# Two attentions as one sequence, heads turned in two places, and other work moved in a four-layer transformer kernel

## The chip, the cores and the metric

The kernel runs on one core of a Trainium2 chip. The metric is the device time of one execution in microseconds. The kernel before took 1555.3 us (median of 3 runs, 1555.01 to 1556.13).

The engines are named as in the profile: PE is TensorE's matmul, PEld its weight load, DVE is VectorE, ACT is ScalarE, POOL is GpSimd, SP is SyncE, which here issues the DMAs.

## The reference, cut to what matters

Four layers run on one sequence of 512 rows of width 1024, in float32. The first two have 256 rows of context beside them and are modulated; the last two each add a gated per-layer embedding.

```python
def ab_layer(...):                                   # layer 1: rows and context together
    h, gate = adaln(x, mod)                          # rmsnorm(x) * (1 + scale) + shift; mod = silu(c) @ mod_w + mod_b
    qa, ka, va, qb, kb, vb, g = heads_ab(h @ w_in, *wts)   # qa, ka = rmsnorm(.., q_gain), rmsnorm([kv[:64], kr], k_gain)
    qa, ka = rope_tail(qa, 32, row, col), rope_tail(ka, 32, row, col)
    qb, kb = axial_rope(qb, row, col), axial_rope(kb, row, col)
    oa = joint_dense_attention(qa, ka, va, kac, vac)  # "mla": 8 heads, 64 + 32 wide; the last 32 of each key are one shared kr
    ob = joint_dense_attention(qb, kb, vb, kbc, vbc)  # "gqa": 8 heads of 64, 2 key heads
    x = x + gate * ((concat(oa, ob) * silu(g)) @ w_out)
# layer 2 ("win"): window attention with a sink, and a short convolution; same frame
# layer 3: 4 heads of a difference of two softmaxes ("diff"), 4 heads with forget gates ("fox"), causal
# layer 4: 8 heads, softmax over a dilated causal pattern ("odd")
def per_layer_embedding(h, p_i, w_ple, w_gate):
    return h + (p_i @ w_ple) * jax.nn.sigmoid(h @ w_gate)
```

## The kernel before, in words

Each engine has its program written out by hand; waits are on semaphores that count up, so an instruction that waits holds up all behind it on its engine. No scheduler moves anything.

A matrix product of two float32 operands is made of three: each operand is split into a high part, rounded to the PE's faster format, and the low rest, and high x high, high x low and low x high are added (L1048 to L1050). ACT makes the high part of a weight tile (L1445) and POOL the low part (L2353), while PE multiplies by the tile before. The rows to be multiplied are turned by PE against a unit matrix (L1004), ACT copies the high part out of PSUM (L1517) and DVE takes the low part (L1959). `turns_at` says beside which weight tile each 128-column slab is turned. Stages follow each other: `in1`, `up`, gqa, mla, `out1`, `in2`, win, `out2`, `in3`, diff and fox, `out3`, `sig3`, `ple3`, `in4`, odd, `out4`, `sig4`, `ple4`.

**Column attention** (gqa, mla, win) goes over units j, one head and one tile of 128 rows each (48, 48 and 32 units). In place j PE makes the scores of unit j (L1269 to L1274), turns what heads are due (L1215, `prep`), turns the probabilities of unit j - 2 (L1236), and in every second place multiplies those of units j - 4 and j - 3 by the values (L1293). DVE finds the maximum (L2093), ACT takes the exponential (L1594), and both copy the turned probabilities out of PSUM (L1610 on ACT, L2104 on DVE). A turned query pair of gqa or win is copied by ACT in two halves (L1572) and its low part taken by DVE in two halves (L2027), all in one place. gqa's places run to 51, the last four without scores, and only then begins mla's place 0. The first head of mla is turned in gqa's last 8 places, and the first of these turns waits until POOL has normed all of mla's queries and keys (`ready_of`, L2400 to L2468).

**mla's norms.** POOL squares each of the six key tiles (L2392, 128x768), DVE sums each (L2252) between its other work of gqa's first six places; there is one buffer for the squares, so the two take turns. The queries' squares and sums are DVE's alone, before gqa. After the root (in gqa's places 6 to 9) POOL multiplies the queries by root and gain and rotates them, then the keys.

**Modulation.** 32 column tiles of `mod_w` are multiplied beside `in1` (L1151) and turned back (L1159), two for each weight tile; ACT copies the results in `mod_columns`. The gates that come of them are spread over a tile by PE (L1168, `spread_at`) in stated places.

**Layer 3** runs its 32 units in `pair_attention`: scores of unit n (L1364, L1371) in PSUM banks 0 and 1 or 2 and 3 by turns, probabilities of unit n - 3 (L1391), values of unit n - 4 (L1401). It begins with a wait for all values of diff and fox; `attention`, for layer 4, likewise. In two late places of fox, slabs 0 and 1 of `m3`, the operand of `out3`, are turned (`late_turn`), slabs 2 to 7 beside `out3`'s first three weight tiles.

Of the kernel before, what the change touches and what calls it, by code (L numbers as in the profile page):

```python
# [108 lines left out]
def build(nc, io, out, known):  # L109
# [22 lines left out]
    with ctx:  # L132
# [145 lines left out]
        def mod_tile(n_):  # L278

            return rx[:, n_ % 4, :].rearrange("p (k m) -> p k m", k=KT)  # L280

        def mod_row(n_):

            return rx[:, NX, n_ % 2 * P:(n_ % 2 + 1) * P]

        def mods_beside(n_):

            return (2 * n_ - 8, 2 * n_ - 7) if 4 <= n_ < 4 + len(MOD) // 2 else ()
# [63 lines left out]
        def lo_of(u):  # L352
# [3 lines left out]
                     ("win", 3): (1, 0, 0), ("win", 9): (1, 0, 1)}  # L356
# [50 lines left out]
        for name, t_ in (("in2", "h2"), ("out3", "m3"), ("out4", "m4")):  # L407
            for u in range(-1 if t_[0] == "h" else 0, 3):
                turns_at[name, 0, u] = [(t_, 2 * u + 2, 2 * u + 4, XT) if t_ == "h2" else (t_, 2 * u + 2, 2 * u + 4)]
# [7 lines left out]
        late_turns = {"fox": "m3", "odd": "m4"}  # L417

        def late_turn(name, j):
# [3 lines left out]
            groups = groups_of(late_turns[name], 0, 2)  # L423
            n_ = j - (len(units_of(name)) - 1 - len(groups))
# [10 lines left out]
        for name in turn:  # L435
            for k in range(turn[name]["slabs"]):
# [3 lines left out]
                for i, g in enumerate(turn[name]["groups"]):  # L440
                    if name[0] == "m" and k < 2:
                        bank_of[name, k, g[0]] = 7
                        continue
# [149 lines left out]

        def pair_done(name, p_):

            return ("mixed", (name, (p_ + 1) * (4 if name == "win" else 6) - 1))
# [15 lines left out]
        def pair_probs(n_, m, a, b):  # L612

            if PAIR[n_][0] == "fox":
                return both_low[:, 2 + n_ % 4, a:b]
            return both[:, 2 * (n_ % 4) + m, a:b]

        def pair_bank(n_):

            return 1 if PAIR[n_][0] == "fox" and n_ % 2 else 6  # L620

# [52 lines left out]
        def prep_times(name):  # L674
# [3 lines left out]
            for p_ in preps:  # L678
# [84 lines left out]
        def heads_view(ap, h):  # L763
            return ap.rearrange("p (h d) -> p h d", h=h)

# [105 lines left out]
        def _(eng):  # L871
# [60 lines left out]
            for m, u in enumerate(first_two[4:], 4):  # L932
# [4 lines left out]
                for n_ in mods_beside(m - 2):  # L937
# [52 lines left out]
        def _(eng):  # L990
# [154 lines left out]
            def modulation_tile(n_):  # L1145

                eng.wait_ge(*at(f"load_mod{n_ % 4}", n_))
                bank_free(7)
                for k in range(KT):
                    q = 32 * (k % 4)  # L1150
                    mm = eng.matmul(psum[q:q + 32, 7, 0:P], silu_pad[:, k, :], mod_tile(n_)[:, k, :], start=k < 4, stop=k >= 4)  # L1151
                mm.then_inc(*to("mod_product", n_))
                reader[7] = ("mod_rows", n_)

            def turn_modulation(n_):

                eng.wait_ge(*at("mod_rows", n_))
                bank_free(7)
                eng.matmul(psum[:, 7, 0:2], mod_row(n_), sel[:, :], start=True, stop=True).then_inc(*to("mod_turned", n_))  # L1159
                reader[7] = ("mod_columns", n_)  # L1160
# [22 lines left out]
            def running_sums():  # L1183
# [11 lines left out]
                "gqa": [("keys_twice", ("gqa", 1))] + [("vector", ("normed", "gq", t)) for t in ALL],  # L1195
                "mla": [("gpsimd", ("normed", n_, t)) for n_ in ("mq", "mk") for t in ALL] + [evac_of("up3", t) for t in ALL],
                "win": [("keys_twice", ("win", 1))] + [("vector", ("normed", "wq", t)) for t in XT],
# [5 lines left out]
            def prep(name, p_):  # L1203

                key, _, rows, tiles, _, d = p_
                if p_[0] == prep_times(name)[-1][0][0]:
                    for w_ in ready_of[name]:
                        eng.wait_ge(*at(*w_))
                if name == "odd" and key[1] == 4:
                    for t in XT:  # L1210
                        eng.wait_ge(*at("vector", ("normed", key[0] + "1", t)))
                b, m_ = prep_bank(name, p_), turned_rows(name, p_)
# [4 lines left out]
                reader[b] = copied(name, p_)  # L1217

# [27 lines left out]
            def column_attention(name):  # L1246
                units, preps = units_of(name), prep_times(name)
                n_units, waited = len(units), set()
                for j in range(n_units + 3):
                    if j < n_units:  # L1250
                        h, t = units[j]
                        wait_heads(name, j, waited)
# [29 lines left out]
                    if 2 <= j < n_units + 2:  # L1282
                        turn_probs(name, j - 2, probs(name, j - 2))
                    m, r = divmod(j - 4, 2)
# [1283 lines left out]
```

## Time and profile before

| what | value |
|---|---|
| median of 3 runs | 1555.3 us |
| the profiled execution's own time | 1554.78 us |
| its span | 1553.0 us |
| PE busy | 1487.5 us, 96% |
| PEld busy | 1240.5 us, 80% |
| DVE, ACT, POOL busy | 850.9, 677.9, 592.3 us |
| mean granted TensorE clock | 0.998 |
| chain that ended last: PE, DVE, POOL, ACT | 81%, 7%, 5%, 3% |

The span runs from the program's first instruction to its last, and 1.8 us of the execution lie around it. Busy is time in which at least one instruction of the engine is under way. PE is idle for 1553.0 - 1487.5 = 65.5 us; the rest of this document is about where.

### The profile page before, as it was taken

How to read it: one execution, taken by the hardware profiler on the slowest of the kernel's cores; microseconds unless marked ns; L12 is line 12 of the kernel's file. 1: busy time of each engine (PE TensorE's matmuls, PEld its weight loads, DVE VectorE, ACT ScalarE, POOL GpSimd, SP SyncE). 2: the span in 40 equal slices, each digit the busy share in tenths (PEclk: the TensorE clock that was granted, in tenths of full speed). 3: DMA queues.
4: the chain of work that ended last, by engine and by line, in shares of the span. 5: the costliest groups of instructions: out<-in, count | busy, mean ns of one | idle time of the engine just before them, and what ended most of it. 6: DMA issues, size and time to landing. Idle time of an engine off the chain costs nothing.

```text
span 1553.0 us, 25078 instructions
## 1 busy us (share of the span) xinstructions
PE 1487.5 (96%) x9488; PEld 1240.5 (80%) x9488; DVE 850.9 (55%) x1879; ACT 677.9 (44%) x1377; POOL 592.3 (38%) x349
## 2 busy tenths in 40 slices
PE   4999998898999999999899999999999999999998
PEld 3778787787888878888788889967788788877887
DVE  4573708876764265933742997056322599617322
ACT  3333336565566353335744333467323433346332
POOL 1212223691005553447725444423234444430244
PEclk9999999999999999999999999999999999999999
DMA  9657620000012333331013323300233233310322
GB/s 326 181 140 192 175 62 27 2 2 1 2 35 89 108 109 96 95 95 42 28 33 94 96 82 98 93 14 28 69 93 106 75 99 101 96 41 1 109 82 95
DMA packets 103717, 128.61 MB, mean 83 GB/s; under 512 B 10608, under 2 KB 63792, under 8 KB 103600
## 3 DMA queue, kind: packets, MB, share of 16 engines
q1 hardware_dynamic: 103600, 127.01, 27.4%
q8 instruction: 78, 1.28, 0.4%
q14 instruction: 39, 0.32, 0.1%
HBM read 124.90 MB, written 2.10 MB: 82 GB/s over the span
## 4 chain that ended last, share of the span: by engine, by line
PE 81%; DVE 7%; POOL 5%; ACT 3%; issue 3%; DMA 1%; SPq 1%; DVEq 0%; ACTq 0%; POOLq 0%
PE psum L1048 21%; PE psum L1050 20%; PE psum L1049 20%; PE psum L1293 3%; PE psum L1236 3%; PE psum L1004 2%; PE psum L1215 2%; PE psum L1151 1%; PE psum L1340 1%; PE psum L1322 1%; PE psum L1272 1%; POOL rx L2403 1%; POOL mla_q L2403 1%; DVE psum L1943 1%; PE psum L1273 1%
## 5 line engine op out<-in xcount | busy, mean ns | idle before, releaser
L2353 POOL TENSOR_TENSOR wlo<-wraw,whi 128x1024 fp32r<-128x1024 f32 (+4 forms) x181 | 413.1, 2283 | 704.6 <-ACT whi L1445 704.6
L1445 ACT ACTIVATE whi<-wraw 128x1024 fp32r<-128x1024 f32 (+4 forms) x181 | 181.6, 1003 | 421.7 <-PE psum L1050 415.4
L1048 PE MATMUL psum<-whi,h2h 128*128 128x512 f32 (+2 forms) x800 | 309.5, 387 | 2.6 <-DVE h2l L1959 1.5
L1050 PE MATMUL psum<-whi,h2l 128*128 128x512 f32 (+2 forms) x800 | 305.2, 382 | 0.0
L1049 PE MATMUL psum<-wlo,h2h 128*128 128x512 f32 (+2 forms) x800 | 304.6, 381 | 0.0
L1048 PEld LDWEIGHTS psum<-whi,h2h 128*128 128x128 f32 x800 | 150.3, 188 | 28.5 <-issue 2.7
L1050 PEld LDWEIGHTS psum<-whi,h2l 128*128 128x128 f32 x800 | 150.2, 188 | 27.1
L1049 PEld LDWEIGHTS psum<-wlo,h2h 128*128 128x128 f32 x800 | 150.4, 188 | 24.8
L1048 PE MATMUL psum<-whi,hTh 128*128 128x512 f32 (+2 forms) x372 | 143.4, 385 | 3.7 <-DVE hTl L1959 2.7
L1050 PE MATMUL psum<-whi,hTl 128*128 128x512 f32 (+2 forms) x372 | 136.2, 366 | 0.0
L1049 PE MATMUL psum<-wlo,hTh 128*128 128x512 f32 (+2 forms) x372 | 135.8, 365 | 0.0
L1048 PE MATMUL psum<-hTh,whi 128*128 128x512 f32 (+1 forms) x288 | 109.0, 379 | 0.8 <-ACT rz L1501 0.8
L1049 PE MATMUL psum<-hTl,whi 128*128 128x512 f32 (+1 forms) x288 | 105.6, 367 | 0.0
L1050 PE MATMUL psum<-hTh,wlo 128*128 128x512 f32 (+1 forms) x288 | 105.4, 366 | 0.0
L2093 DVE TENSOR_REDUCE nmax<-psum 128x1 f32<-128x768 f32 (+1 forms) x96 | 74.9, 780 | 49.6 <-PE psum L1274 28.2
L1048 PEld LDWEIGHTS psum<-whi,hTh 128*128 128x128 f32 x372 | 70.5, 189 | 18.0 <-POOL wlo L2353 4.6
L1594 ACT ACTIVATE pr<-psum,nmax 128x768 f32<-128x768 f32 (+3 forms) x96 | 64.1, 667 | 39.2 <-DVE nmax L2093 23.7
L1050 PEld LDWEIGHTS psum<-whi,hTl 128*128 128x128 f32 x372 | 70.3, 189 | 11.5
L2364 POOL TENSOR_TENSOR hTl<-rz,hTh 128x768 fp32r<-128x768 f32 (+1 forms) x12 | 19.7, 1647 | 156.4 <-ACT hTh L1616 156.4
L1049 PEld LDWEIGHTS psum<-wlo,hTh 128*128 128x128 f32 x372 | 70.7, 190 | 9.1
L1959 DVE TENSOR_TENSOR h2l<-psum,h2h 128x512 fp32r<-128x512 f32 x32 | 22.0, 691 | 86.0 <-ACT h2h L1517 85.9
L1236 PE MATMUL psum<-ident,pr 128*128 128x128 f32 x368 | 58.8, 277 | 6.1 <-ACT prT L1610 1.8
(391 smaller groups left out, 2956.4 us busy)
## 6 DMA issues: line engine op xcount, KB each, us to landing
rx<-mod_w_in SPq DMA_DIRECT2D x32, 512.0 KB, 5.1
wraw<-w_in_odd_in SPq DMA_DIRECT2D x32, 512.0 KB, 3.6
wraw<-cd_w_in_in SPq DMA_DIRECT2D x24, 512.0 KB, 3.7
wraw<-w_in_even_in SPq DMA_DIRECT2D x20, 512.0 KB, 3.7
wraw<-ab_w_out_in SPq DMA_DIRECT2D x16, 512.0 KB, 3.7
wraw<-w_ple_gate_in SPq DMA_DIRECT2D x16, 512.0 KB, 3.8
mod_w_even<-mod_w_in SPq DMA_DIRECT2D x8, 512.0 KB, 10.3
wraw<-ab_w_in_in SPq DMA_DIRECT2D x8, 512.0 KB, 8.3
```

Source lines behind the costliest of these rows:

```text
L1004: mm = eng.transpose(psum[:, b, n_ * P:(n_ + 1) * P], turn[name]["rows"](t, k), ident[:, :])
L1048: eng.matmul(dst, a[0], ww[0], start=first, stop=False)
L1049: eng.matmul(dst, a[0], ww[1], start=False, stop=False)
L1050: mm = eng.matmul(dst, a[1], ww[0], start=False, stop=last_)
L1215: mm = eng.transpose(psum[0:m_, b, n_ * P:(n_ + 1) * P], rows(t), ident[:, :])
L1236: mm = eng.transpose(psum[:, bk, (b - b0) * P:(b - b0 + 1) * P], place[:, b * P:(b + 1) * P], ident[:, :])
L1293: eng.matmul(psum[64 * e:64 * e + 64, 6, 0:P], v_rows(name, h + e, b), turned_probs(name, 2 * m + e)[:, n_ * P:(n_ + 1) * P], start=n_ == ...
L1445: eng.activation(hi_of(u)[:, :, 0:w], wraw[:, u["id"] % RAW, :, 0:w], ACT.Copy).then_inc(*to("split_hi", u["id"]))
L1594: eng.activation(place[:, 0:w], psum_flat[:, s0 * 512:s0 * 512 + w], ACT.Exp, bias=nmax[:, j % 4:j % 4 + 1], scale=-1.0, accum_out=rsum[:, ...
L2093: eng.tensor_reduce(m, sc, AX.X, ALU.min).then_inc(*note("nmax", (name, j)))
L2353: eng.tensor_tensor(lo_of(u)[:, :, 0:w], wraw[:, u["id"] % RAW, :, 0:w], f32(hi_of(u)[:, :, 0:w]), ALU.subtract)\
L2403: eng.tensor_tensor(view(t), view(t), gg, ALU.mult).then_inc(*(small() if turned else note("gpsimd", ("normed", name, t))))
```

## The change

In the order of the program:

- **Modulation.** The last two of the 32 column tiles leave `in1`; they are multiplied in gqa's places 0 and 1 and turned back in places 1 and 2. `mod_columns` is split into `mod_rows` and `mod_columns`.
- **First heads.** A head's turn waits for its own norms: gqa's and win's keys for `keys_twice` alone, mla's keys and queries each for their own.
- **mla's norms.** The shared 32 columns of a key are squared once; the other 64 of 8 heads in twelve pieces of 128x256 with two buffers, of which DVE sums two in each of six places. The gain of the keys' first 64 columns is multiplied into the queries' gain, so POOL multiplies only 32 columns of each key head by a gain (128x256 in place of 128x768). Keys are normed before queries.
- **One sequence.** gqa and mla form one list of places: mla's place 0 follows gqa's place 47. Heads 2 and 3 of mla are turned in places 3 to 10 (before: 0, 1, 3, 4, 6, 7, 9, 10).
- **Pairs.** The second half of a turned query pair is copied and its low part taken one place after the first.
- **Gate.** Layer 2's gate, second half, is spread in win's place 6 (before: 9).
- **Values.** diff, fox and odd wait for their values just ahead of the first product with them.
- **fox.** Its scores go through banks 0, 2 and 3. Slabs 0 to 3 of `m3` are turned in four late places, slabs 4 to 7 beside `out3`'s first two weight tiles.

```diff
         def mods_beside(n_):
-            return (2 * n_ - 8, 2 * n_ - 7) if 4 <= n_ < 4 + len(MOD) // 2 else ()
+            return mod_pair(n_) if n_ < 19 else ()
...
         spread_at = {("gqa", 5): (0, 0, 0), ("gqa", 7): (0, 0, 1), ("gqa", 9): (0, 1, 0), ("gqa", 21): (0, 1, 1),
-                     ("win", 3): (1, 0, 0), ("win", 9): (1, 0, 1)}
+                     ("win", 3): (1, 0, 0), ("win", 6): (1, 0, 1)}
...
+        for u in range(2):
+            turns_at["out3", 0, u] = [("m3", 2 * u + 4, 2 * u + 6)]
...
-        late_turns = {"fox": "m3", "odd": "m4"}
+        late_turns, EARLY_SLABS = {"fox": "m3", "odd": "m4"}, {"m3": 4, "m4": 2}
...
+        def places(*names):
+            return [(name, j) for name in names for j in range(len(units_of(name)) + 4 * (name == names[-1]))]
...
+        def pair_scores(n_):
+            return 2 * (n_ % 2) if PAIR[n_][0] == "diff" else (0, 2, 3)[(n_ - 16) % 3]
...
-                    when = first + (3 * before // 2 if name == "mla" else 2 + 2 * before)
+                    when = first + (max(3 * before // 2, 3 + before if first == 0 else 0) if name == "mla" else 2 + 2 * before)
...
+            def start_modulation(j):
+                if j < 2:
+                    modulation_tile(30 + j)
+                if j > 0:
+                    turn_modulation(29 + j)
...
-                if p_[0] == prep_times(name)[-1][0][0]:
+                if name in STACKED and key[1] == 0:
+                    for w_ in [("keys_twice", (name, 1))] if key[0] == "k" else [("vector", ("normed", name[0] + "q", t)) for t in tiles]:
+                        eng.wait_ge(*at(*w_))
+                elif p_[0] == prep_times(name)[-1][0][0]:
...
+                if name == "mla" and key[1] == 0:
+                    for t in tiles:
+                        eng.wait_ge(*at("gpsimd", ("normed", "m" + key[0], t)))
...
                         bl = blocks_of(name, t)
+                        if i == 0:
+                            values_ready(name)
                         copies_ready(name, i)
...
             def column_attention(*names, beside):
...
                     if j < len(units_of(name)):
                         maximum(name, j)
+                    for what in preps_at(name, j - 1) if j else ():
+                        low(*what, which=(1,))
                     for what in preps_at(name, j):
-                        low(*what)
+                        low(*what, which=(0,))
...
             def mla_norms():
...
+                eng.tensor_tensor(shared_squares, kr[:, :, :], kr[:, :, :], ALU.mult).then_inc(*note("squares_g", ("kr", 0)))
+                for n_ in range(2 * NT):
...
+                    eng.tensor_tensor(key_squares(n_), rows, rows, ALU.mult).then_inc(*note("squares_g", ("mk", n_)))
                 eng.wait_ge(*at("vector", ("root", "mla")))
-                for name, roots in (("mq", heads_rstd[:, 0:48]), ("mk", heads_rstd[:, 48:96])):
+                for name, roots in (("mk", heads_rstd[:, 48:96]), ("mq", heads_rstd[:, 0:48])):
...
-            column_attention("gqa")
-            column_attention("mla")
+            column_attention("gqa", "mla")
```

What this makes of the instructions' order is shown at three places. PE at gqa's start, before (kTs and qTs are gqa's turned keys and queries, gq its rows, pr the probabilities):

```order
L1269 MATMUL psum<-kTs,qTs 128x512
L1270 MATMUL psum<-kTs,qTs 128x512
L1269 MATMUL psum<-kTs,qTs 128x256
L1270 MATMUL psum<-kTs,qTs 128x256
L1269 MATMUL psum<-kTs,qTs 128x512
L1270 MATMUL psum<-kTs,qTs 128x512
L1269 MATMUL psum<-kTs,qTs 128x256
L1270 MATMUL psum<-kTs,qTs 128x256
L1269 MATMUL psum<-kTs,qTs 128x256
L1270 MATMUL psum<-kTs,qTs 128x256
L1215 MATMUL psum<-ident,gq 128x128 x4
L1236 MATMUL psum<-ident,pr 128x128 x6
```

and now, from the end of the first unit's scores:

```order
L1323 MATMUL psum<-kTs,qTs 128x256
L1186 MATMUL psum<-rx,silu_pad 32x128 x8
L1322 MATMUL psum<-kTs,qTs 128x512
L1323 MATMUL psum<-kTs,qTs 128x512
L1322 MATMUL psum<-kTs,qTs 128x256
L1323 MATMUL psum<-kTs,qTs 128x256
L1186 MATMUL psum<-prT,silu_pad 32x128 x8
L1195 MATMUL psum<-sel,prT 128x2
L1322 MATMUL psum<-kTs,qTs 128x256
L1323 MATMUL psum<-kTs,qTs 128x256
L1262 MATMUL psum<-ident,gq 128x128 x4
L1195 MATMUL psum<-sel,prT 128x2
```

The two modulation tiles (L1186) and their turns (L1195) stand among the first three units' scores. ACT a few instructions later, before (more_q is a turned query pair's place, prT and rx the turned probabilities):

```order
L1594 ACTIVATE pr,rsum<-psum,nmax 128x768 x2
L1572 ACTIVATE more_q<-psum 64x512 x2
L1610 ACTIVATE prT<-psum 128x512
L1594 ACTIVATE rx,rsum<-psum,nmax 128x256
L1610 ACTIVATE prT<-psum 128x512
L1594 ACTIVATE pr,rsum<-psum,nmax 128x256
L1572 ACTIVATE more_q<-psum 64x256 x2
```

and now:

```order
L1770 ACTIVATE modc<-psum,mod_b 128x2
L1628 ACTIVATE more_q<-psum 64x512
L1666 ACTIVATE prT<-psum 128x512
L1650 ACTIVATE rx,rsum<-psum,nmax 128x256
L1628 ACTIVATE more_q<-psum 64x512
L1666 ACTIVATE prT<-psum 128x512
L1650 ACTIVATE pr,rsum<-psum,nmax 128x256
L1628 ACTIVATE more_q<-psum 64x256
L1650 ACTIVATE pr,rsum<-psum,nmax 128x768
L1628 ACTIVATE more_q<-psum 64x256
```

Each second half now stands behind an exponential and a copy. PE at the end of gqa, before (kTh, kTl, qTh, qTl are mla's turned keys and queries, high and low; the products with the values that stand between are left out):

```order
L1215 MATMUL psum<-ident,mla_q 96x128 x2
L1236 MATMUL psum<-ident,pr 128x128 x12
...
L1298 MATMUL psum<-ident,rinv 64x128 x2
L1236 MATMUL psum<-ident,rx 128x128 x6
...
L1272 MATMUL psum<-kTh,qTh 128x512
```

and now:

```order
L1262 MATMUL psum<-ident,mla_q 96x128 x2
L1289 MATMUL psum<-ident,pr 128x128 x6
L1325 MATMUL psum<-kTh,qTh 128x512
L1326 MATMUL psum<-kTl,qTh 128x512
L1327 MATMUL psum<-kTh,qTl 128x512
...
L1289 MATMUL psum<-ident,pr 128x128 x6
...
L1354 MATMUL psum<-ident,rinv 64x128 x2
```

mla's first scores stand between the turned probabilities of gqa's last units.

## Rows read from the trace of the kernel before

**Rows 1.** Busy time by stretch: length, busy of each engine, clock, DMA.
```profile
262.00:294.00 32.00, 24.83 (x214) 20.33 (x216) 26.81 (x58) 17.56 (x40) 11.50 (x9) 1.00 0.01 2
```

**Rows 2.** Waits of PE, whole span: us in total, times, longest.
```profile
PE psum L1215 <- DVE nlam L2235: 1.6, 1, 1.6
...
PE psum L1048 <- DVE h2l L1959: 1.5, 1, 1.5
PE psum L1215 <- POOL rx L2403: 1.4, 1, 1.4
PE psum L1364 <- ACT buf L1501: 1.4, 1, 1.4
...
PE psum L1322 <- ACT buf L1501: 1.3, 1, 1.3
...
PE psum L1168 <- DVE kTw L2027: 1.1, 1, 1.1
```

**Rows 3.** Timeline of PE in in1: start, us, what, idle before.
```profile
197.37 0.40 PE L1049 MATMUL psum<-hTl,whi 128*128 128x512 f32 x1
197.60 0.40 PE L1050 MATMUL psum<-hTh,wlo 128*128 128x512 f32 x1
197.93 0.64 PE L1151 MATMUL psum<-rx,silu_pad 128*32 128x128 f32 x16
198.50 0.38 PE L1048 MATMUL psum<-hTh,whi 128*128 128x256 f32 x1
```

**Rows 4.** Timeline of DVE ahead of gqa's first maximum.
```profile
259.45 2.31 DVE L2027 TENSOR_TENSOR qTs<-psum,qTs 64x512 fp32r<-64x512 f32 x4
263.10 0.96 DVE L2093 TENSOR_REDUCE nmax<-psum 128x1 f32<-128x768 f32 x1 [1.33 <-PE psum L1270]
```

**Rows 5.** Groups of DVE, 262 to 294: busy, mean ns, idle before.
```profile
L2252 DVE TENSOR_REDUCE ssq<-squares 128x8 f32<-128x768 f32 x6 | 5.7, 953 | 1.9 <-POOL squares L2392 1.5
...
L2093 DVE TENSOR_REDUCE nmax<-psum 128x1 f32<-128x256 f32 x4 | 1.7, 425 | 0.4
```

**Rows 6.** Timelines of DVE and of POOL beside each other in in3.
```profile
864.67 0.69 DVE L1857 TENSOR_REDUCE ssq<-squares 128x8 f32<-128x512 f32 x1
865.46 1.98 DVE L1855 TENSOR_TENSOR squares<-buf 128x512 f32<-128x512 f32 x1
...
864.13 2.76 POOL L2353 TENSOR_TENSOR wlo<-wraw,whi 128x1024 fp32r<-128x1024 f32 x1 [3.55 <-ACT whi L1445]
```

**Rows 7.** Timeline of PE: a wait in gqa, two in win.
```profile
308.68 1.01 PE L1236 MATMUL psum<-ident,rx 128*128 128x128 f32 x6 [0.64 <-ACT prT L1610]
...
750.72 0.52 PE L1236 MATMUL psum<-ident,win_pr 128*128 128x128 f32 x3 [0.89 <-ACT gate L1610]
...
760.57 0.41 PE L1236 MATMUL psum<-ident,win_pr 128*128 128x128 f32 x2 [0.71 <-ACT win_prT L1610]
```

**Rows 8.** Groups of POOL, 250 to 355.
```profile
L2403 POOL TENSOR_TENSOR rx<-rx,gains 128x768 f32<-128x768 f32 x6 | 11.0, 1826 | 0.5
...
L2392 POOL TENSOR_TENSOR squares<-rx 128x768 f32<-128x768 f32 x6 | 8.8, 1467 | 17.2 <-DVE ssq L2252 17.2
...
L2461 POOL TENSOR_TENSOR squares<-rx,grid 128x128 f32<-128x128 f32 x4 | 1.8, 457 | 0.3
```

**Rows 9.** Waits of PE, 371 to 387, from gqa's end into mla.
```profile
PE psum L1293 <- DVE rz L2123: 1.1, 1, 1.1
PE psum L1272 <- ACT pr L1594: 0.6, 1, 0.6
PE psum L1236 <- ACT prT L1610: 0.6, 1, 0.6
```

**Rows 10.** Timelines of POOL and PE: sub-norms' end, fox's twelfth scores' end.
```profile
1082.94 1.28 POOL L2450 TENSOR_TENSOR rz<-rz 128x512 f32<-128x512 f32 x1
...
1085.24 0.22 PE L1373 MATMUL psum<-mask_right,mask_left 128*128 128x128 f32 x1
```

**Rows 11.** Busy time by stretch, near the start.
```profile
26.00:29.00 3.00, 3.00 (x9) 2.31 (x9) 0.00 (x0) 1.06 (x1) 0.14 (x1) 0.50 1.07 361
```

More of the change, by code:

```diff
@@ L1244, in copies_ready, with column_attention @@
                     eng.wait_ge(*at("probs_b", (name, i)))
[L1246 to L1250, printed above, removed]
+            def column_attention(*names):
+                seq, waited = places(*names), {name: set() for name in names}
+                for n_, (name, j) in enumerate(seq[:-1]):
+                    units = units_of(name)
+                    if j < len(units):
                         h, t = units[j]
-                        wait_heads(name, j, waited)
+                        wait_heads(name, j, waited[name])
                         s0 = score_bank(j)
@@ L1345, in pair_attention @@
             def pair_attention():
-                for name in ("diff", "fox"):
-                    for n_ in values_of[name]:
-                        for t in XT:
-                            eng.wait_ge(*at(*evac_of(n_, t)))
                 waited = set()
@@ L1571, in prep @@
                 for e, (rows, hi, _) in enumerate(parts_of(name, p_)):
+                    if e not in which:
+                        continue
                     eng.activation(hi, shaped(psum[rows, prep_bank(name, p_), 0:len(tiles) * P], hi), ACT.Copy)\
@@ L1616, in mix_hi, with column_attention @@
                 eng.activation(hi, m, ACT.Copy).then_inc(*to("mix_hi", (name, p_)))
[L1618 to L1620 removed]
+            def column_attention(*names):
+                seq = places(*names)
+                if "gqa" in names:
+                    mod_rows(30)
+                for n_, (name, j) in enumerate(seq):
+                    units = units_of(name)
                     if (name, j - 1) in spread_at:
                         spread(*spread_at[name, j - 1])
+                    for what in preps_at(name, j - 1) if j else ():
+                        prep(*what, which=(1,))
                     for what in preps_at(name, j):
[L1624 to L1626 removed]
+                        prep(*what, which=(0,))
+                    if 2 <= n_ < len(seq) - 2:
+                        copy_probs(*seq[n_ - 2], turned_probs(*seq[n_ - 2]), product_of(seq[n_ - 5]) if n_ >= 5 else None)
                     if j < len(units):
[L1628 to L1629 removed]
+                        if n_ >= 3:
+                            probs_free(*seq[n_ - 3])
                         exponentials(name, j, probs(name, j))
+                    if name == "gqa" and j < 2:
+                        if j == 0:
+                            mod_rows(31)
+                        mod_columns(30 + j)
                     if (name, j) in LEADS:
@@ L1757, in _ @@
             products("in1", "up", beside=tables)
-            column_attention("gqa")
-            column_attention("mla")
+            column_attention("gqa", "mla")
             def first_squares(where):
@@ L2104, in copy_probs, with column_attention @@
                 eng.tensor_copy(place[:, 0:nb * P], psum[:, 4, 0:nb * P]).then_inc(*note("probs_a", (name, i)))
-            def column_attention(name, beside=lambda j: None):
-                units, preps = units_of(name), prep_times(name)
-                for p_ in preps[-1] if name == "win" else ():
-                    first_head(name, p_)
-                for j in range(len(units) + 4):
-                    if j < len(units):
+            def column_attention(*names, beside):
+                seq = places(*names)
+                for p_ in prep_times("win")[-1] if "win" in names else ():
+                    first_head("win", p_)
+                for n_, (name, j) in enumerate(seq):
+                    if j < len(units_of(name)):
@@ L2129, in column_attention @@
-                    beside(j)
+                        eng.reciprocal(rinv[:, r_:r_ + 2], rsum[:, c_:c_ + 2]).then_inc(*note("vector", ("inverse", name2, m)))
+                    if name != "mla":
+                        beside(j)
             def attention(name):
@@ L2283, in _ @@
                     first_head("gqa", p_)
-            column_attention("gqa", mla_norms)
-            column_attention("mla")
+            column_attention("gqa", "mla", beside=mla_norms)
             products("out1", 0)
@@ L2306, in conv @@
                        .then_inc(*note("conv", ("lo", c)))
-            column_attention("win", conv)
+            column_attention("win", beside=conv)
             products("out2")
```

170 lines of the change are left out of this document (104 added, 66 removed).

## The prediction

> **What bounds the kernel now.** I read the page's busy shares first: PE is busy for 1487.5 of 1553.0 us, so all that moving work about can win is the 65.5 us in which it is idle, and what stands in PE's way as surplus. Next the mean clock, 0.998: nearly everything runs at the upper level. Next the busy time by stretch, to find the idle time. It isn't in the weight products but at the borders of the attentions, and the worst stretch is the first 32 us of gqa, where PE is busy for 24.8 us and DVE for 26.8 [rows 1]: there DVE sets the pace. Last the waits of PE, whose single large ones [rows 2] I take one by one, since the change names most of them.
>
> **The change part by part.** Each term is a gain of PE's time.
>
> *Modulation and first heads.* A modulation tile in `in1` stands between starts at 197.60 and 198.50, where two matmuls follow each other after 0.23 us: 0.90 - 0.23 = 0.67 us of PE [rows 3]. Two tiles leave, 1.3 us; their turns, a matmul of two columns each, I count at nothing. In gqa's places 0 and 1 the tiles cost nothing, as PE waits there for DVE and ACT. ACT's two copies and two column results fall between exponentials that wait for maxima. The first turn of gqa's keys no longer waits for the queries' norms, 1.6 us [rows 2]. But both come to PE's queue before gqa, and ahead of the first scores DVE has a chain of its own, which ends with the low part of the queries at 259.45 + 2.31 = 261.76 and is then idle for 1.33 us, until the first maximum [rows 4]. That chain is led by work that follows PE in `up`, so it moves with the 1.3 us. Of the 1.6 us only what lies between 261.76 and the scores' start is left: two matmuls of 512 and two of 256 columns and a hand-over take about 1.0 of the 1.33 us, so 0.3. Term: 1.6 us. Bounds: 0.3 if DVE's chain doesn't move, 2.9 if it is no limit.
>
> *mla's norms at gqa's start.* DVE waited 1.5 us in all for POOL's squares [rows 5]; with two buffers POOL works ahead. Its pieces of 256 columns take between 0.46 and 1.47 us [rows 8], two in each place, so 2.9 us at most where a place of this stretch takes over 2. DVE sums twelve pieces at 0.43 (the price of a 128x256 reduction) = 5.1 us in place of 5.7, and adds one more sum and one addition, at most 0.43 each, and six more hand-overs at about 0.07 ((1.9 - 1.5) / 6) = 0.4 [rows 5]. So 1.5 + 0.6 - 0.7 - 0.4 = 1.0 us. Bounds: 0 and 2.
>
> What could eat this is POOL itself, which now squares while DVE sums; before, one buffer kept them apart. In `in3` both occur beside each other: with POOL at work from 864.13 to 866.89, DVE's product of two tiles in SBUF takes 1.98 us, until about POOL's end, while its reduction in the same stretch takes 0.69 [rows 6]. The Trainium skill, page "SBUF — State Buffer", section on the shared port pair, has it that a VectorE instruction with two SBUF inputs and a GpSimd instruction that reads SBUF shut each other out for their whole length, and that a reduction on trn2 never contends; the trace agrees. By the rule alone the twelve sums keep their 0.43 us. Were it wrong, each sum would wait for up to a piece of POOL's.
>
> *POOL's chain.* PE waits 1.4 us for it at mla's first turn [rows 2]. Twelve gain products of 1.83 us stood in the chain; six shrink to 256 columns, between 0.46 and 1.83 us each [rows 8], and nearest to 0.7 by a straight line: the chain is 6 x 1.1 = 6.8 us shorter. Keys come first and only they are waited for in gqa's place 40. The whole 1.4 us goes. Bounds: 0.9 and 1.6. Next late is the PSUM bank between the turns, which is not changed.
>
> *The seam.* From gqa's end into mla PE waits 1.1 us for DVE's mixing, 0.6 for ACT's copy and 0.6 for the first exponential of mla [rows 9]. They come of draining one list and filling another. In one sequence mla's scores stand between gqa's last turned probabilities, so 2.3 us go. Against it mla's turns for heads 2 and 3 now fall in eight places in a row, which hand one bank on each time: I give back 0.4. Term 1.9. Bounds: 0 and 3.
>
> *Pairs.* Where a query pair is copied in two halves the turned probabilities stand behind 1.2 us of ACT. PE waited 0.64, 0.89 and 0.71 us at three such places [rows 7], 2.2 in all; smaller ones follow them. Half a copy later takes half the delay away, and the other half falls in a place that has its own slack: 1.5 us. Bounds: 0 and 3.
>
> *Gate.* At win's place 9 PE waits 1.1 us for the bank of a key's turn [rows 2]; in place 6 the bank is free, as the last turn before it is in place 1, with its second half in place 2. All of it: 1.1. Bounds 0.5 and 1.1.
>
> *Values.* PE waits 1.4 us before diff and 1.3 before odd for ACT's last copy of values [rows 2]. Scores and maximum now run beside ACT's copies, and the first exponential comes as ACT is done. Term 2.4 of 2.7. Bounds 1.0 and 2.7.
>
> *m3.* `out3` waits 1.5 us for the low part of slabs 2 and 3 [rows 2], turned beside its first tile. They now come in fox's late places. Slabs 4 and 5, due two weight tiles later, have a tile's four row tiles of time (4 x 6 matmuls at 0.23 = 5.5 us). Term 1.5. The first late turn is one place earlier, and needs POOL's sub-norms, which ended at 1084.22, while PE had that place's scores done at 1085.46 [rows 10]: 1.2 us of cover, enough. If it is gone, the wait is the difference. The third bank of fox I count at nothing. Bounds 0.5 and 2.0.
>
> Sum: 1.6 + 1.0 + 1.4 + 1.9 + 1.5 + 1.1 + 2.4 + 1.5 = 12.4 us. The profiled execution took 1554.8 us, so 1542.4; the median is 0.5 above it, and I say **1542.5 us**. All lower ends together give 1554.8 - 3.2 = 1551.6, all upper ends 1554.8 - 18.3 = 1536.5. Nothing behind a term can swallow it, since weight products follow, in which PE is never idle for long and transfers run far ahead.
>
> **The rivals.**
>
> *A. The gains are swallowed where DVE sets the pace.* In gqa's first 32 us DVE has 26.8 us of work [rows 1], and the halves' later places are full too. Then modulation, norms and pairs give 1.0 together in place of 4.1, and the seam half, 1.0 in place of 1.9. For it: that stretch; against it: elsewhere DVE is busy half the time. 12.4 - 3.1 - 0.9 = 8.4, time 1546.5.
>
> *B. More is hidden than the rows show.* PE's matmuls overlap, so a wait shorter than one's own 0.4 us is not idle time [rows 3]. A smoother sequence would win such waits too. If each of mla's and win's 80 units won 0.05 us, 4 us more: 1538.5.
>
> *C. Waits only change their names.* Each wait removed lets another, just behind, stand in its place. For it: some of them have a second releaser close by. Against it: those of [rows 2] have different places and partners, with whole stages between. 1554 us.
>
> *D. Slower: the clock falls at gqa's start.* PE now comes to the first scores up to 1.3 us sooner than DVE's chain lets it go on, just ahead of a stretch with 7 us of idle time. Near the start, where PE had waited for DVE, the granted clock was 0.50 for 3 us [rows 11], the level of 1.2 GHz. The page "TensorE: Matmul & The Clock Gate" of the Trainium skill, part on the warmup, says that the clock follows how busy the PE has lately been; by it the modulation tiles in that gap speak against a fall. If all of the stretch's 24.8 us of PE work ran at half speed, it would take 24.8 us more, less the 7 us idle, 17.8 in all: 1542.5 + 17.8 = 1560. It decides from 12 us of loss, that is when some 19 us of work run at the lower level. Against it: the stretch was granted 1.00 [rows 1].
>
> *E. POOL holds DVE's sums* (the rule above wrong): twelve sums each up to 0.7 us longer, 8 us at worst, but half overlaps: 1546.5, the time of A.
>
> **How the numbers follow.** Forecast 0.60 (its own range 1539 to 1546), A and E 0.19, B 0.10, C 0.06, D 0.05. The range that holds 8 in 10 reaches to B's 1538.5 and below it to the upper bounds' 1536.5, and up over A to 1550.5, just short of the lower bounds' end. A change of 0.2%, 3.1 us, is about what a measurement of this kernel tells from none: faster by more than that in all of the forecast, A, B and E, 0.89; within it C, 0.06; slower D, 0.05.
>
> **What the profile of the changed kernel would show.** PE busy for 1486 us or less of a span of about 1541; no wait of PE for `nlam`, for POOL at mla's first turn, for `kTw` at the gate, or for ACT's values ahead of diff and odd; the first weight product of `out3` after its turned tiles without idle time; POOL's norms done some 9 us sooner (6.8 + 1.6 + 1.0); DVE's wait for squares gone; mla's first scores ahead of gqa's last product. Wrong would be a granted clock under 1.00 around 260, a new wait of PE for a turned head in mla's places 3 to 10, or one for DVE in the second of a pair's two places.

## The result and the profile after

The kernel after takes 1547.56 us (median of 4 runs, 1546.89 to 1548.31) where the kernel before took 1555.21 beside it: ratio 0.9950, 95% interval 0.9933 to 0.9967. It is 7.65 us faster. I had said 12.7 us, so the time lies in the range and beyond the likeliest case's own range of 1539 to 1546. The profiled execution took 1546.89 us, its span is 1545.1 us, PE is busy for 1488.6 us, DVE 852.2, ACT 679.4, POOL 586.1, and the mean clock is 0.997.

To see where time went I took the start of the same matmul in both traces, before less after, at the borders of stretches. Between two borders the difference is what the stretch gained or lost.

| stretch (us before) | PE's lead at its end | gained | my term |
|---|---|---|---|
| start to 200 | -0.16 | -0.2 | |
| modulation and first heads, to 256 | 2.85 | 3.0 | 1.6 |
| gqa to 352: norms, pairs there | -1.12 | **-4.0** | 1.0 and a part of 1.5 |
| POOL's wait, at 354 | 0.45 | 1.6 | 1.4 |
| seam, to 400 | 2.46 | 2.0 | 1.9 |
| mla, rest of layer 1 | 2.24 | -0.2 | |
| win: gate, pairs there | 4.45 | 2.2 | 1.1 and a part of 1.5 |
| in3 | 4.01 | -0.4 | |
| values (diff 1.4; odd 1.45 less 0.7 given back) | | 2.2 | 2.4 |
| fox ahead of its late turns | | 1.4 | 0 |
| m3, late turns and out3 | | 1.2 | 1.5 |

The table adds up to 8.8 us, and the span is only 7.9 us shorter: 0.9 us are lost behind PE's last matmul. The result leaves in four transfers, and the last of them landed 3.2 us after its issue and lands after 4.1 now. The rows for the tile `out`, before, then after:

```profile
DMA to landing us min/median/max: 2.6/2.9/3.3
```

```profile
DMA to landing us min/median/max: 2.7/3.0/4.1
```

From DVE's last instruction to the end of the span it is 3.7 us in the kernel before and in the one variant built on it, and 4.6 us in all twelve executions of the kernel after and its variants. In the twelve, and in neither of the two, a packet of 8192 bytes of the instruction queue (q14) falls into that transfer, whose last packets then come one after another. That this packet is the cause fits all fourteen traces, but no run tests it.

All but one of the stretches up to PE's last matmul came near or above what I had said. One, gqa, lost 4.0 us where it was to win some 2. The 0.4 us of in3 is no effect of the change: of twelve profiled executions of the kernel after and its variants, five have this step of 0.44 us and seven don't, and none of the edits touches in3. The waits of PE in the kernel after, whole span, as in [rows 2]:

```profile
PE psum L1262 <- DVE more_q L2096: 2.2, 3, 1.2
PE psum L1211 <- DVE more_q L2096: 2.2, 1, 2.2
PE psum L1289 <- DVE prT L2173: 1.4, 2, 1.1
PE psum L1211 <- DVE qTs L2096: 1.4, 1, 1.4
...
PE psum L1262 <- DVE kTs L2096: 0.7, 1, 0.7
```

Those of [rows 2] for `nlam`, POOL, ACT's values, `kTw` and `h2l` at out3 (1.5) are gone. Four of the lines shown are new. Two are gate spreads (L1211) and one is turns (L1262), and these wait for the low part of a turned pair. The fourth, for `kTs`, stands before gqa, where the first turn of the queries waits for the low part of the keys. The timeline of PE in gqa's places 4 to 6, and one later spread for comparison:

```profile
268.90 0.44 PE L1262 MATMUL psum<-ident,gq 128*128 128x128 f32 x2 [1.16 <-DVE more_q L2096]
...
272.65 0.41 PE L1289 MATMUL psum<-ident,pr 128*128 128x128 f32 x2 [0.23 <-DVE rx L2173]
275.21 1.96 PE L1211 MATMUL psum<-ident,modc 128*128 128x128 f32 x8 [2.15 <-DVE more_q L2096]
276.82 0.56 PE L1322 MATMUL psum<-kTs,qTs 128*128 128x256 f32 x1
...
278.80 0.32 PE L1349 MATMUL psum<-rx,gq 128*64 128x128 f32 x1
...
280.60 1.06 PE L1211 MATMUL psum<-ident,modc 128*128 128x128 f32 x8
```

The spread of place 5 waits 2.15 us, and then its eight matmuls take 1.96 us where the next spread's take 1.06. DVE in that place, and PE's clock by stretch (columns as in [rows 1]):

```profile
272.61 0.94 DVE L2334 TENSOR_REDUCE ssq<-squares 128x4 f32<-128x256 f32 x2
273.65 0.96 DVE L2162 TENSOR_REDUCE nmax<-psum 128x1 f32<-128x768 f32 x1
274.64 0.43 DVE L2096 TENSOR_TENSOR more_q<-psum,more_q 64x256 fp32r<-64x256 f32 x1
275.10 0.42 DVE L2173 COPY prT<-psum 128x256 f32<-128x256 f32 x1
```

```profile
262.00:294.00 32.00, 26.71 (x238) 22.29 (x231) 25.98 (x64) 18.01 (x43) 11.63 (x19) 0.95 0.01 2
...
274.00:276.00 2.00, 0.79 (x4) 0.82 (x5) 1.87 (x5) 0.99 (x2) 0.56 (x1) 0.83 0.00 0
276.00:278.00 2.00, 2.00 (x11) 2.00 (x11) 1.65 (x6) 0.60 (x1) 0.00 (x0) 0.50 0.00 0
278.00:280.00 2.00, 2.00 (x20) 1.51 (x19) 0.90 (x4) 1.05 (x3) 0.00 (x0) 0.82 0.01 4
```

The reader is to see two things. The second half's low part (274.64) stands behind two norm sums and the next unit's maximum, though its bank could have been free a place earlier. And behind PE's wait the granted clock was 0.50, the level of 1.2 GHz, for some 3 us. In [rows 1] it was 1.00 in the same stretch.

### The profile page after: what moved, and what is told of

Read it like the earlier page. It is cut to its first block, busy times and chain, and to the rows that moved or that the text cites. A ratio compares the mean times of both kernels' runs of the same rounds, so it can differ in the third digit from the quotient of the medians.

```text
span 1545.1 us, 25132 instructions
## 1 busy us (share of the span) xinstructions
PE 1488.6 (96%) x9488; PEld 1242.6 (80%) x9488; DVE 852.2 (55%) x1888; ACT 679.4 (44%) x1377; POOL 586.1 (38%) x356
## 4 chain that ended last, share of the span: by engine, by line
PE 85%; DVE 7%; ACT 3%; issue 3%; POOL 1%; DMA 1%; SPq 1%; DVEq 0%; ACTq 0%
PE psum L1082 21%; PE psum L1084 20%; PE psum L1083 20%; PE psum L1349 5%; PE psum L1289 4%; PE psum L1038 2%; PE psum L1262 2%; PE psum L1322 1%; PE psum L1396 1%; PE psum L1186 1%; PE psum L1376 1%; PE psum L1325 1%; PE psum L1323 1%; PE psum L1354 1%; PE psum L1327 1%
## 5 line engine op out<-in xcount | busy, mean ns | idle before, releaser
L1082 PEld LDWEIGHTS psum<-hTh,whi 128*128 128x128 f32 x288 | 54.3, 188 | 11.7 <-issue 3.8
```

The costliest lines, as they stand in the source:

```text
L1082: eng.matmul(dst, a[0], ww[0], start=first, stop=False)
```

## The experiments

**Which part of gqa's loss is the split?** Four kernels. In the first and the last, pairs are split in one attention only:

```diff
-                    for what in preps_at(name, j - 1) if j else ():
+                    for what in preps_at(name, j - 1) if j and name in SPLIT_IN else ():
                         prep(*what, which=(1,))
                     for what in preps_at(name, j):
-                        prep(*what, which=(0,))
+                        prep(*what, which=(0,) if name in SPLIT_IN else (0, 1))
```

and the same for `low` on DVE. Whole in gqa (`SPLIT_IN = ("win",)`):

> The changed kernel with gqa's turned pairs copied whole in one place again (win's stay split). Theory T (the held bank): the second half keeps PSUM bank 7 a place longer, and the gate spreads of gqa's places 5 and 21 and the pair turned in place 4 wait for it. Then PE's waits of 2.15, 1.38 and 1.16 us at these three go, and 3 to 4.5 us come back: 1543 to 1544.5. Rival P (DVE sets the pace there, whatever the order): the same DVE work remains, waits change their names, under 1 us comes back: 1546.5 to 1547.5. Rival M (the loss is from the two modulation tiles and ACT's copies for them among the first scores): nothing comes back, 1547.5, or 0.5 us slower since the halves no longer relieve ACT.

Measured: 1541.87 us (1541.48 to 1542.54), ratio to before 0.9912 (0.9898 to 0.9925). By matmuls compared with the kernel after, 4.6 us come back between 264 and 334 us, more than T's 3 to 4.5. Besides, there are 0.2 us before it, 0.3 in mla, which no edit explains, and 0.5 at the step of in3. Theory T holds for the place of the loss and the waits that go. PE and DVE there:

```profile
272.62 0.41 PE L1290 MATMUL psum<-ident,pr 128*128 128x128 f32 x2 [0.57 <-DVE rx L2174]
272.86 1.06 PE L1212 MATMUL psum<-ident,modc 128*128 128x128 f32 x8
273.68 0.36 PE L1323 MATMUL psum<-kTs,qTs 128*128 128x256 f32 x1
...
274.96 0.44 PE L1290 MATMUL psum<-ident,pr 128*128 128x128 f32 x2 [0.36 <-DVE prT L2174]
275.57 0.29 PE L1350 MATMUL psum<-rx,gq 128*64 128x128 f32 x1 [0.18 <-DVE rz L2195]
```

```profile
271.13 0.88 DVE L2097 TENSOR_TENSOR more_q<-psum,more_q 64x256 fp32r<-64x256 f32 x2
...
273.62 0.96 DVE L2163 TENSOR_REDUCE nmax<-psum 128x1 f32<-128x768 f32 x1
```

Both halves are done by 272.01, so the spread runs at once, while DVE is at its sums and its maximum. The clock is 1.00 all through 262 to 294. From the spread's start to the first product with values it takes 275.57 - 272.86 = 2.71 us, of which 0.54 are waits, 2.17 of work; in the kernel after 278.80 - 275.21 = 3.59. So of the 4.6 us some 1.4 are the clock's.

**Gate spreads in even places**, pairs still split: `("gqa", 5), 7, 9, 21` become `6, 8, 10, 22`.

> The changed kernel with layer 1's gate spread in gqa's places 6, 8, 10 and 22 (as changed: 5, 7, 9, 21), pairs still split. Theory T: in place 6 and 22 the second half has left bank 7, so the waits of 2.15 and 1.38 us go, while that of 1.16 us at the pair turned in place 4 stays: 2.5 to 3.5 us come back, 1544 to 1545. Rival P (DVE sets the pace): under 1 us, 1546.5 to 1547.5. Rival M (the modulation tiles): nothing, 1547.5.

Measured: 1545.19 us (1545.05 to 1546.65), ratio 0.9934 (0.9922 to 0.9947); in the trace 1.5 us come back. Less than T said. The clock stays at 1.00, but the wait changes its name:

```profile
275.51 0.44 PE L1289 MATMUL psum<-ident,pr 128*128 128x128 f32 x2 [1.84 <-DVE prT L2173]
```

```profile
273.58 0.96 DVE L2162 TENSOR_REDUCE nmax<-psum 128x1 f32<-128x768 f32 x1
274.57 0.42 DVE L2096 TENSOR_TENSOR more_q<-psum,more_q 64x256 fp32r<-64x256 f32 x1
275.03 0.42 DVE L2173 COPY prT<-psum 128x256 f32<-128x256 f32 x1
```

In the kernel after DVE had to wait for the slowed PE just behind this place, 0.84 + 0.33 + 0.23 = 1.4 us:

```profile
278.90 0.42 DVE L2173 COPY prT<-psum 128x256 f32<-128x256 f32 x1 [0.84 <-PE psum L1289]
...
280.14 0.42 DVE L2162 TENSOR_REDUCE nmax<-psum 128x1 f32<-128x256 f32 x1 [0.33 <-PE psum L1323]
280.80 0.42 DVE L2173 COPY rx<-psum 128x256 f32<-128x256 f32 x1 [0.23 <-PE psum L1289]
```

Here it does not, so nearly all of the 1.5 us is the clock's, and taking the spreads off the held bank won next to nothing by itself. I read it so: DVE sets the pace, and what counts is which work of PE stands ahead of its wait for DVE. When the spread is free to go in place 5, as with whole pairs, its 0.8 us and the next scores run while DVE is busy; in place 6 it comes after the wait and adds to it. No run tests this reading alone.

**The split alone, on the kernel before:**

> The kernel before with the split of pairs alone, in gqa and win. Theory T: PE loses 3 to 4.5 us by gqa's place 24 against the kernel before and wins about 1 us in win: 1557 to 1558.5. My forecast's own term (pairs win 1.5 us): 1553.8. Rival P (DVE sets the pace, order indifferent): 0.5 us lost in gqa, 1 us won in win, 1554.8.

Measured: 1556.01 us (1555.33 to 1557.48), ratio 1.0002 (0.9993 to 1.0011). In the trace it loses 4.1 us between 264 and 334 us, gets 1.6 back at 354, where PE waited for POOL anyway [rows 2], and wins 1.8 in win. That is T's loss, but T's time was 1 us too high, since it had not seen that POOL's wait would hide a part. The medians alone would not tell the split from nothing. T's waits and the slow clock appear here too, with no modulation tile about, so the tiles are not the cause (rival M). Waits of PE, then the clock:

```profile
PE psum L1168 <- DVE more_q L2033: 2.2, 1, 2.2
...
PE psum L1168 <- DVE qTs L2033: 1.4, 1, 1.4
```

```profile
278.00:280.00 2.00, 1.67 (x8) 1.70 (x9) 1.80 (x6) 0.81 (x2) 0.39 (x1) 0.54 0.03 8
280.00:282.00 2.00, 2.00 (x14) 1.83 (x15) 0.91 (x3) 0.91 (x2) 0.00 (x0) 0.61 0.01 4
```

**Whole in win, split in gqa:**

> The changed kernel with win's turned pairs copied whole in one place again (gqa's stay split). Layer 2 of the changed kernel is 2.2 us shorter, of which the gate's place should be 1.1 and the split 1.1. If so, 1.1 us is lost in win: 1548.7. If the gate's place alone made the 2.2 us, 1547.5; if the split made all of it, 1549.7.

Measured: 1549.35 us (1548.92 to 1549.66), ratio 0.9958 (0.9945 to 0.9972). In the trace win loses 1.9 us, all that the split could have made there and more than the 1.6 us of the two rows of win in [rows 7].

**Single parts taken back from the kernel after.** The yardstick is another set of runs of the kernel after:

> The changed kernel itself, nothing edited, as the yardstick for runs that differ by under 1 us: 1547 to 1548.5. In the trace the stretch of in3 (930 to 950 us) should be 0.4 to 0.6 us shorter than in the first trace of it, as in all four variants of it, and no DVE or PE wait of the attentions should move by more than 0.1 us.

Measured: 1547.31 us (1546.49 to 1548.18). The low clock is there again, 276 to 281 us. The step in in3 did not go, against what I had expected; no wait of the attentions moved. The traces also differ by 0.7 to 1.2 us at about 31 us, where the modulation weights come in, so I compare within stretches only. A part that is worth less than 1 us can't be told by these medians, but by the trace.

The gate again in win's place 9 (`("win", 6)` to `("win", 9)`):

> The changed kernel with layer 2's second gate half spread in win's place 9 again. My forecast had 1.1 us for this move; but win is only 2.2 us shorter, and copying win's pairs whole cost 1.9 of these. Theory T2 (PE's wait of 1.1 us in place 9 was for DVE, which the later matmuls of the place would have waited for anyway): 0.3 us is lost in win, 1547.9 to 1548.4 where the changed kernel takes 1547.6 to 1548.2. Forecast's term: 1.1 us lost, 1548.7 to 1549.3.

Measured: 1547.99 us; win loses 0.33 us in the trace. PE's old wait is back with its full length, and yet the move was worth a third of it. In the kernel after five short waits stand at 738 to 748 us that this run does not have, of 0.28, 0.18, 0.10, 0.13 and 0.20 us, 0.9 in all, mostly for DVE's copies and mixing. They take the rest, as T2 said. The old wait:

```profile
PE psum L1211 <- DVE kTw L2096: 1.1, 1, 1.1
```

fox's scores in two pairs of banks (`return 2 * (n_ % 2)` for all units):

> The changed kernel with fox's scores in two pairs of banks by turns again (0 and 2 in place of 0, 2 and 3). I had counted the third bank at nothing. The stretch of fox is 1.4 us shorter in the changed kernel. Theory F (PE no longer waits for the exponential of two units before): 1.0 to 1.4 us are lost within fox, 1548.7 to 1549.5. Rival V (the 1.4 us come of the values wait moved behind the first scores): nothing is lost, 1547.6 to 1548.2.

Measured: 1548.02 us; in the trace 1.0 us is lost between 1068 and 1071 us and 0.2 of it won back. Theory F, a little below its range. That leaves 0.6 of fox's 1.4 us, whose cause stays open. PE in that trace waits for the exponential of two units before:

```profile
1069.83 1.10 PE L1423 MATMUL psum<-kT,qT 128*128 128x512 f32 x2 [0.74 <-ACT both_low L1753]
```

m3's slabs 2 and 3 beside out3 again:

```diff
-        late_turns, EARLY_SLABS = {"fox": "m3", "odd": "m4"}, {"m3": 4, "m4": 2}
+        late_turns, EARLY_SLABS = {"fox": "m3", "odd": "m4"}, {"m3": 2, "m4": 2}
```

> The changed kernel with only slabs 0 and 1 of m3 turned in fox's late places and 2 to 7 beside out3's first three weight tiles, as before. My term: 1.5 us lost at out3's start, 1549.1 to 1549.7. From the two traces out3's start gained 1.2 us: 1548.8 to 1549.4. If the low part of slabs 4 and 5 is now late in place of that of 2 and 3, under 0.5 us is lost, 1548.5 or less.

Measured: 1547.40 us; in the trace 1.6 us go out of fox's end, 2.7 come in at out3, 1.1 net. The wait of 1.5 us for `h2l` is back. The medians don't show it.

The first turn waits for the queries' norms again:

```diff
-                    for w_ in [("keys_twice", (name, 1))] if key[0] == "k" else [("vector", ("normed", name[0] + "q", t)) for t in tiles]:
+                    if p_[0] != prep_times(name)[-1][0][0]:
+                        w_all = []
+                    else:
+                        w_all = [("keys_twice", (name, 1))] + [("vector", ("normed", name[0] + "q", t)) for t in (ALL if name == "gqa" else XT)]
+                    for w_ in w_all:
```

> The changed kernel with the first turn of gqa's and win's keys waiting for the queries' norms too, as before. My forecast gave this part 0.3 us at gqa's first maximum, since DVE's own chain was to end there last. The traces say 2.9 us in all for this and the two modulation tiles. Theory K (the low parts of the keys stand ahead of those of the queries in DVE's queue, so the whole chain starts with the keys' turn): 1.3 to 1.6 us are lost by gqa's first maximum, 1548.9 to 1549.7. Theory of the forecast: 0.3 us, 1547.9 to 1548.5.

Measured: 1547.89 us. In the trace PE loses 1.80 us at the keys' turn, and 1.05 us of them still at gqa's first maximum. Neither theory: DVE's own chain does end there last, as I had said, and the keys' low parts don't wait. DVE and POOL in this kernel, then in the kernel after:

```profile
247.21 3.00 DVE L2361 TENSOR_TENSOR squares<-mla_q 128x768 f32<-128x768 f32 x1
...
246.99 2.40 POOL L2451 TENSOR_TENSOR wlo<-wraw,whi 128x1024 fp32r<-128x1024 f32 x1 [7.86 <-ACT whi L1502]
```

```profile
246.41 1.96 DVE L2357 TENSOR_TENSOR squares<-mla_q 128x768 f32<-128x768 f32 x1
...
244.39 3.16 POOL L2447 TENSOR_TENSOR wlo<-wraw,whi 128x1024 fp32r<-128x1024 f32 x1 [6.06 <-ACT whi L1498]
```

The squares of a query tile, a product of two SBUF inputs, take 0.96 us elsewhere in this row of norms. These begin beside POOL's last low part of a weight and end 0.82 us behind its end in both kernels (250.21 and 249.39; 248.37 and 247.55): they are held until POOL is done. The two traces are 0.80 us apart before the stretch, and by so much DVE's squares begin apart. POOL begins 2.60 us apart, since its input follows PE's place in `up`; in the kernel after it takes 3.16 us in place of 2.40, as it begins 0.06 us behind DVE's product before (244.33, 0.96 us), so its ends are 1.84 us apart. So the collision is 1.04 us shorter when PE goes on without the wait. That is what the first heads won, by a neighbour I had not looked at. The rule of the Trainium skill that I cited (page "SBUF — State Buffer", section "Who interferes with whom") describes this case, and the trace agrees.

**Other ways to cut a pair, and DVE's sums.** Both halves in one place, around the copy of the turned probabilities (on ACT; on DVE likewise):

```diff
                     for what in preps_at(name, j):
                         prep(*what, which=(0,))
                     if 2 <= n_ < len(seq) - 2:
                         copy_probs(...)
+                    for what in preps_at(name, j) if name != "win" else ():
+                        prep(*what, which=(1,))
```

> The changed kernel with gqa's pairs copied in two halves in one place, the first ahead of the turned probabilities' copy, the second right behind it, on ACT and DVE alike (win's as changed). It is to keep what the split was for and give back the bank within the place. Theory T (what cost was the hold over the place's end): at least as good as copying whole, and the 1.4 us for which PE then waits for ACT's copy behind both halves shrinks by 0.6: 1541 to 1542 where copying whole took 1541.9. Rival T' (any delay of the bank's release costs, since the spreads come next): the second half is 0.6 us (ACT) and 0.4 us (DVE) later than when copied whole, at six pairs: 1543 to 1545. If the split itself costs, whatever its distance: near 1547.

Measured: 1542.48 us (1541.47 to 1542.92), ratio 0.9913 (0.9900 to 0.9927): the same as whole. In the trace 0.3 us better. The spread of place 5 now starts at once, behind a second low part that ends within the place:

```profile
273.63 1.13 PE L1211 MATMUL psum<-ident,modc 128*128 128x128 f32 x8
...
273.05 0.43 DVE L2098 TENSOR_TENSOR more_q<-psum,more_q 64x256 fp32r<-64x256 f32 x1
```

What costs in gqa is the hold over the place's end, not the cut.

DVE's twelve sums over nine places, pairs whole in gqa:

```diff
-                if j < NT:
+PIECES = (2, 2, 1, 1, 1, 1, 1, 1, 2)
...
+                if j < len(PIECES):
...
-                    reduce_keys(2 * j)
-                    reduce_keys(2 * j + 1)
+                    for n_ in range(sum(PIECES[:j]), sum(PIECES[:j + 1])):
+                        reduce_keys(n_)
```

> Gqa's pairs copied whole, and DVE's twelve sums of mla's key squares spread over nine places (2, 2, 1, 1, 1, 1, 1, 1, 2) in place of two in each of six, the roots three places later. Theory S (DVE sets the pace in gqa's places 2 to 6, where PE still waits 0.64, 0.57, 0.36 and 0.29 us for DVE's copies): 0.47 us less of DVE in each of four places, 1 to 2 us gained against copying whole: 1540 to 1541. Rival Q (POOL's chain, then about 8 us later, holds the first turn of mla's queries, which had some 9 us of cover): nothing gained or up to 2 us lost, 1542 to 1544.

Measured: 1541.00 us (1540.27 to 1541.71), ratio 0.9905 (0.9891 to 0.9918); in the trace 1.8 us better than whole. Theory S. PE is busy for 29.16 of the first 32 us, against 26.71 in the kernel after:

```profile
262.00:294.00 32.00, 29.16 (x270) 23.98 (x270) 28.19 (x71) 20.53 (x47) 8.03 (x12) 1.00 0.01 2
```

Both together:

> The changed kernel with gqa's pairs copied in halves around the turned probabilities' copy, within one place, and DVE's twelve key sums spread over nine places. The one gave 0.3 us in the trace against copying whole, the other 1.8. With the sums out of the way, DVE no longer holds what ACT's earlier copy frees, so the sum should be 2 us or a little more by gqa's place 12: 1540.5 to 1541.3, that is 0.3 to 0.7 us below the spread sums alone (1541.0), at the edge of what the runs can tell. Rival: the second low part, now behind DVE's copy, is as late as before and holds the bank, and nothing is gained over the spread sums: 1541 or 0.3 above.

Measured: 1540.52 us (1539.65 to 1541.08), ratio 0.9904 (0.9887 to 0.9920). It is the fastest of all, though not told apart from the spread sums alone; in the trace it is 0.2 us better in gqa. The kernel after stood at 0.9944 (0.9930 to 0.9957) in its longer set of runs, so these two edits win some 6 us over it.

## Why the prediction was right in its range and wrong in its size

*The sum.* The profiled execution missed by 1546.9 - 1542.4 = 4.5 us. Pairs came out 4.2 us worse than their term and the last transfer took 0.9 us more, while all other stretches together were 0.6 us better than said. That they so nearly cancelled is luck: modulation was off by +1.4 us, the gate by -0.8, and fox won 1.4 that I had not counted.

*What bounds the kernel.* Right in that the waits at the attentions' borders were worth taking one by one, and the worst stretch, gqa's first 32 us, is where the forecast failed. "Nothing behind a term can swallow it" was wrong: I looked at the weight products alone, and 0.9 us went at the last transfer, a place that the sum did not have.

*Modulation and first heads,* 1.6 said, 3.0 measured, just above the upper bound of 2.9. The two tiles with their turns were 1.9 to 2.1, not 1.3: I had counted the turns at nothing. The first heads gave 1.05, not 0.3, by POOL's collision. DVE's chain did move with PE.

*mla's norms,* 1.0 said, about 0.6 measured. Mechanism right: DVE's wait for squares is gone, and each sum takes 0.42 us beside POOL's squares and is not held by them (E fell):

```profile
L2334 DVE TENSOR_REDUCE ssq<-squares 128x4 f32<-128x256 f32 x12 | 5.0, 420 | 1.2
```

The size is read with pairs whole in gqa, where the next item can't cover it: PE's lead over the kernel before grows there from 3.1 us at 256 to 3.7 at 352. No run takes the norms alone.

*Pairs.* **This step failed.** The term was 1.5 us; measured are 1.9 in win and -4.6 in gqa, -2.7 in all, 4.2 us from the term, against a miss of 5.1 in the whole. The words of it that failed: "the other half falls in a place that has its own slack". In gqa's places 3, 5 and 21 it has none: DVE reaches the second half only behind sums and a maximum, and a gate spread or the next turn in PE's queue needs the bank that it holds. PE stopped there for 1.16, 2.15 and 1.38 us, and the clock's fall behind the second made it 1.4 us more. The first of these waits cost nothing in the end: by 272.65 the kernel after had caught up with the one whose pairs are whole. The diff showed both lists of places, and I looked for the wait in mla's places only. The lower bound of 0 was wrong too: a part that is moved later can cost, and nothing excluded it.

*POOL's chain,* 1.4 said, 1.6 measured. The last of its products ends at 343.86 + 1.84 = 345.70, against 353.71 before: 8 us sooner, where I had said 9. *The seam,* 1.9 said, 2.0 measured; the waits there are now, where [rows 9] had 1.1, 0.6 and 0.6:

```profile
PE psum L1262 <- DVE more_q L2096: 1.1, 2, 0.9
PE psum L1289 <- ACT rx L1666: 0.2, 1, 0.2
```

The first of them is the 0.4 I had given back, sized too low and paid by the rest; it is also the wait for a turned head among mla's places that I had named as a sign of being wrong. *Gate,* 1.1 said, 0.33 measured, below its lower bound: the wait came back with its whole length in that run and cost a third of it. The rest went to the five short waits behind it. *Values,* 2.4 said, 2.2 measured. *m3,* 1.5 said, 1.2 measured by the traces and 1.1 by its own run, since the two slabs' turns don't come quite for nothing in fox. *The third bank of fox,* nothing said, 0.8 measured (1.0 less the 0.2 won back).

*Rivals.* A had the right place and the right sign of the miss (1546.5), but not its cause. D came true in small: the clock fell not at 260 but at 275, behind a wait that the change itself had made, for 3 us and not 25, and it cost 1.4 us. C's mechanism shows at the gate and in the even places, where waits changed their names, but not in the whole. B's small waits can't be told from the rest. The sign of being wrong that the trace showed most plainly was the wait for DVE in the second of a pair's two places. PE busy was to be 1486 or less and is 1488.6. The half clock is not the whole reason, as two variants without it have 1488.4 and 1488.0 (halves around the copy, sums spread) and one has 1486.4 (pairs whole).

What stays open, beside the last transfer: how near the other kernels were to the clock's fall. It stood in all eight executions with gqa's split and the spread in place 5 (the kernel after twice, the split on the kernel before, whole in win, and the four single parts) and in none of the five other variants, nor in the kernel before.

## What to carry to other kernels

An operand that is copied later holds its buffer longer. Before cutting a copy in two, look for the next user of the bank in the queue of the engine that fills it, and for what stands ahead of the second half on the engine that empties it. Where one engine sets the pace, first thin out its own movable work there: spreading twelve reductions over three more places won more than the cleverest cut.

## What the runs showed of the hardware that I had not expected

PE's clock dropped from 1.00 to 0.50 for some 3 us in the middle of an attention, behind a wait of 2.15 us that followed shorter ones of 0.54, 0.63, 1.16 and 0.23; with waits of 0.53, 0.64, 1.16, 0.22 and 1.84 us (spreads in even places) it did not. So a wait can cost more than its own length, and which side of the border a kernel is on is to be read in the clock by stretch, since the mean over the span (0.997 against 0.998) hides it.

The last transfer of the result took 3.2 us from its issue to its landing in both kernels without the change and 4.1 us in all twelve with it, though its issue and size are the same. The waits of PE don't show this; the end of the span behind the last instruction of DVE does.
